# Residual columns summed by TensorE behind a normed result, the residual's update as two scalings and two adds on GpSimd

## What is computed

```python
for l in range(DEPTH):                                   # DEPTH = 2
    h = swiglu(rms_norm_2(x, ng[0]), ffn_w_gate[l, 0], ffn_w_up[l, 0], ffn_w_down[l, 0])
    x = x + 0.5 * rms_norm_2(h, ng[1])
    h = rms_norm_2(x, ng[2])
    ...
    x = x + rms_norm_2(h, ng[3])
    h = memory_xattn(rms_norm_2(x, ng[4]), mem_n, xa_wq[l], xa_wk[l], xa_wv[l], xa_wo[l])
    x = x + rms_norm_2(h, ng[5])
    h = swiglu(rms_norm_2(x, ng[6]), ffn_w_gate[l, 1], ffn_w_up[l, 1], ffn_w_down[l, 1])
    x = x + 0.5 * rms_norm_2(h, ng[7])
```

## Time and profile before

| | |
|---|---|
| median of 3 runs | 3472.39 us (3471.25 to 3475.31) |
| the profiled execution | 3471.19 us |
| its span | 3469.4 us |
| mean granted clock of TensorE | 0.918 of full speed |
| busy | PE 83%, PEld 65%, DVE 71%, ACT 22%, POOL 18% |
| HBM | 247 GB/s over the span |

### The profile page before, as it was taken

One profiled execution on the slowest core, in us unless ns is written; L12 is line 12 of the kernel. 1 busy time (PEld: TensorE's weight loads), 2 busy tenths in 40 slices (PEclk: granted clock), 3 DMA queues, 4 the chain that ended last, 5 costly groups with the idle time before them and its releaser, 6 DMA issues. The chain is left out here.

```text
span 3469.4 us, 44826 instructions
## 1 busy us (share of the span) xinstructions
PE 2896.9 (83%) x17440; PEld 2263.6 (65%) x17440; DVE 2457.6 (71%) x4625; ACT 774.4 (22%) x1982; POOL 626.5 (18%) x520
## 2 busy tenths in 40 slices
PE   8789977777777889677777779997887999998898
PEld 8678963333333689333333329987777899987798
DVE  7261677777777886877777878774436877868786
ACT  4114122222222342122222221013222101023300
POOL 0000014445444100344444440000000000000000
PEclk9899988898888899898888889998989999999999
DMA  6263559999999735899999995643203565652364
GB/s 206 87 190 99 195 209 421 410 417 414 404 401 421 260 113 171 352 414 420 417 406 389 416 391 172 192 149 128 74 5 126 170 191 173 189 172 94 123 193 142
DMA packets 469124, 859.87 MB, mean 248 GB/s; under 512 B 18736, under 2 KB 398512, under 8 KB 402224
## 3 DMA queue, kind: packets, MB, share of 16 engines
q0 software_dynamic: 73728, 536.90, 37.5%
q1 hardware_dynamic: 394896, 319.85, 29.2%
q10 hardware_dynamic: 288, 0.24, 0.0%
HBM read 848.55 MB, written 8.39 MB: 247 GB/s over the span
## 5 line engine op out<-in xcount | busy, mean ns | idle before, releaser
L2435 PE MATMUL banks<-arena,arena 128*128 128x512 f32 x1744 | 922.9, 688 | 344.4 <-ACT arena L2504 344.1
L2435 PEld LDWEIGHTS banks<-arena,arena 128*128 128x128 f32 x1744 | 374.4, 222 | 874.1 <-issue 444.6
L2393 POOL DMA_INDIRECT arena<-in_peer_uv,arena x512 | 621.5, 1214 | 1375.2 <-DVE arena L2621 681.3
L2659 DVE CUSTOM_DVE_ANT_0 arena<-arena,normed 128x1024 f32<-128x1024 f32 x512 | 625.3, 1222 | 229.1 <-DMA arena<-in_peer_uv,arena 227.0
L409 DVE TENSOR_TENSOR weight_ring_part<-weight_ring,weight_high_parts 128x2048 fp32r<-128x2048 f32 (+2 forms) x244 | 539.8, 2212 | 8.3
L3213 PE MATMUL banks<-normed_columns_part,weight_high_parts 128*128 128x256 f32 x1408 | 394.8, 280 | 3.3 <-DVE weight_ring_part L409 2.8
L3214 PE MATMUL banks<-normed_part,weight_high_parts 128*128 128x256 f32 x1408 | 392.6, 279 | 0.0
L3215 PE MATMUL banks<-normed_columns_part,weight_ring_part 128*128 128x256 f32 x1408 | 392.3, 279 | 0.0
L753 PE MATMUL banks<-weight_high_parts,arena_part 128*128 128x256 f32 x1216 | 342.6, 282 | 36.6 <-PEq L349 23.8
L406 DVE CAST weight_high_parts<-weight_ring 128x2048 fp32r<-128x2048 f32 (+2 forms) x244 | 289.6, 1187 | 104.2 <-PE banks L755 83.8
L754 PE MATMUL banks<-weight_ring_part,arena_part 128*128 128x256 f32 x1216 | 340.1, 280 | 0.0
(11 more groups left out here) (569 smaller groups left out, 4283.5 us busy)
## 6 DMA issues: line engine op xcount, KB each, us to landing
weight_ring<-in_ffn_w_gate SPq DMA_DIRECT2D x88, 512.0 KB, 3.7
weight_ring<-in_ffn_w_up SPq DMA_DIRECT2D x88, 512.0 KB, 4.9
weight_ring<-in_ev_w_in SPq DMA_DIRECT2D x33, 1024.0 KB, 5.4
weight_ring<-in_ffn_w_down SPq DMA_DIRECT2D x32, 1024.0 KB, 5.2
weight_ring<-in_od_w_in SPq DMA_DIRECT2D x23, 1024.0 KB, 5.3
weight_ring<-in_xa_wkv SPq DMA_DIRECT2D x16, 1024.0 KB, 5.3
weight_ring<-in_peer_wq SPq DMA_DIRECT2D x16, 1024.0 KB, 5.3
weight_ring<-in_ev_w_out SPq DMA_DIRECT2D x12, 1024.0 KB, 5.8
```

The lines of the kernel that those rows point to most:

```text
L2393: pool.indirect_dma_start(out=ring[:, slot(i, s), :], out_offset=None, in_=table, in_offset=bass.IndirectOffsetOnAxis(ap=index[:, i % 2, s ...
L2435: mm = pe.matmul(k.ps[:, 2 * b + half, :], diag[:, g % 2, s, :], v, start=n == b * PEER_TOPK, stop=n == last_mixed[b])
L2659: dve.tensor_tensor_reduce(out=ring[:, here, 0:D], in0=ring[:, here, 0:D], in1=k.xn[:, i % NB, :], scale=1.0, scalar=0.0, op0=ALU.mult, op ...
```

## The change

TensorE adds up the new columns itself: x turned by a matmul with the identity, plus the result times a diagonal matrix of its scale, in one bank (banks 2 to 5). The first three of four turns of the old x go before the wait for the scale. VectorE makes the two diagonals in place of its L845. GpSimd updates the rows of x once all turns are done: two scalings of `weighted` in place, then two adds, each over 128x1024. `weighted` moves to the arena (after `self.xn`, which now receives low parts while `weighted` is still read). In the next step's first tile, m=0 and m=1 (or both blocks of the first tile in `rows_out`) are made in turns, two chunks each as the parts come, except where `columns_out` has `follows` or `tensor_then`. The last landing keeps the update on VectorE, as two instructions of 128x1024. L827 moves ahead of the wait for the squares.

```diff
@@ land
-        weighted = self.xn[:, :, :].rearrange("p b (h d) -> p (b h) d", d=WIDTH)
+        weighted = self.take(NB * tiles, WIDTH) if post is not None else None
...
+                def turned_piece(t, i, b):
+                    return self.ps[:, TURNS + t, i * T + b * P:i * T + (b + 1) * P]
+                def turn_old(t):
+                    pe.wait_ge(self.squared.sem, self.squared.start + TURNS + t + 1)
+                    for i in range(2):
+                        for b in range(NB):
+                            c = 2 * t + i
+                            pe.matmul(turned_piece(t, i, b), self.x[:, b, c * P:(c + 1) * P], self.c("ident"),
+                                      start=i == 0 and b == 0, stop=False)
+                def turn_result(t):
+                    for i in range(2):
+                        for b in range(NB):
+                            mm = pe.matmul(turned_piece(t, i, b), weighted[:, t * NB + b, i * P:(i + 1) * P],
+                                           self.wide[:, b * P:(b + 1) * P], start=False, stop=i == 1 and b == NB - 1)
+                    mm.then_inc(self.turned.sem, 1)
...
-                    pe.wait_ge(self.landed.sem, self.landed.start + (j + 1) * NB)
-                    if post is not None:
-                        pe.wait_ge(self.squared.sem, self.squared.start + tiles * NB)
-                    self.turn(pe, j)
...
+                    for t in range(tiles - 1):
+                        turn_old(t)
+                    pe.wait_ge(self.tile_out.sem, self.tile_out.start + tiles * NB)
+                    pe.wait_ge(self.norm_diag.sem, self.norm_diag.start + NB)
+                    for t in range(tiles):
+                        if t == 2:
+                            turn_old(tiles - 1)
+                        turn_result(t)
...
+                @block.gpsimd
+                def _(pool):
...
+                    pool.wait_ge(self.turned.sem, self.turned.start + tiles)
+                    for b in range(NB):
+                        rows = weighted.rearrange("p (j b) d -> p b j d", b=NB)[:, b]
+                        pool.tensor_scalar(rows, rows, self.out_scale[:, b:b + 1], None, ALU.mult).then_inc(self.tile_out.sem, 1)
+                    for b in range(NB):
...
+                        pool.wait_ge(self.tile_out.sem, self.tile_out.start + tiles * NB + b + 1)
+                        pool.tensor_tensor(x, rows, x, ALU.add).then_inc(self.landed.sem, tiles)
...
-                for j in range(tiles):
+                if nxt is not None:
                     for b in range(NB):
-                        dve.scalar_tensor_tensor(piece(self.x, j, b), weighted[:, j * NB + b, :], self.out_scale[:, b:b + 1],
-                                                 piece(self.x, j, b), ALU.mult, ALU.add).then_inc(self.landed.sem, 1)
...
+                        dve.tensor_scalar(self.wide[:, b * P:(b + 1) * P], self.c("ident"), self.out_scale[:, b:b + 1], None,
+                                          ALU.mult).then_inc(self.norm_diag.sem, 1)
+                    for t in range(tiles):
+                        self.keep_low(dve, t, nxt, high_out, low_out, TURNS)
+                if nxt is None:
+                    dve.wait_ge(self.tile_out.sem, self.tile_out.start + tiles * NB)
+                    add_result(dve)
@@ columns_out (and alike in ffn, in rows_out by blocks)
+        paired = fresh and not follows and tensor_then is None
...
+                    if fresh and m == 0:
+                        for c in range(0, kc, 2):
                             self.column_ready(pe, c)
+                            for block in range(2 if paired else 1):
+                                product(block, (c, c + 1))
+                    elif not (paired and m == 1):
+                        product(m, range(kc))
                     if fresh and m == 1:
                         self.scale_tensor(pe)
```

More of the change, by code:

```diff
@@ L32 @@
 BANKS = 8
+TURNS = 2
 SIDE_BANKS = 2
@@ L757, in _ @@
                                 mm.then_inc(self.produced.sem, 1)
[L758 to L765 removed]
+                if post is None:
+                    pe.wait_ge(self.landed.sem, self.landed.start + tiles * NB)
+                    self.turn(pe, tiles - 1)
+                elif nxt is not None:
+                    self.behind(pe, self.landed)
+                    for t in range(tiles - 1):
[6 more added lines that the diff above has]
+                        turn_result(t)
@@ L822, in _ @@
                 done = self.vector_done
+                if unscaled:
+                    dve.tensor_scalar(self.out_mean, self.mean, EPS / factor ** 2, None, ALU.mult).then_inc(done.sem, 1)
+                    done.adds(1)
                 dve.wait_ge(self.squared.sem, self.squared.start + tiles * NB)
@@ L857, in land @@
             if post is not None:
-                self.tile_out.adds(NB * tiles)
+                self.tile_out.adds(NB * tiles + (NB if nxt is not None else 0))
                 self.out_ready.adds(1)
@@ L861, in land @@
                 self.out_inverted.adds(1)
+                if nxt is not None:
+                    self.norm_diag.adds(NB)
             if nxt is not None:
@@ L907, in _, with product @@
             def _(pe):
-                for m, (i, j) in enumerate(parts):
+                def product(m, chunks):
+                    i, j = parts[m]
+                    w_high, w_low = self.weights(pe, first + i)
+                    bank, w = self.ps[:, m % banks, 0:T], slice(j * P, (j + 1) * P)
+                    for c in chunks:
+                        pe.matmul(bank, w_high[:, c, w], high[:, c, :], start=c == 0, stop=False)
+                        pe.matmul(bank, w_high[:, c, w], low[:, c, :], start=False, stop=False)
+                        mm = pe.matmul(bank, w_low[:, c, w], high[:, c, :], start=False, stop=c == kc - 1)
+                    if c == kc - 1:
+                        mm.then_inc(self.produced.sem, 1)
+                for m in range(len(parts)):
                     if tensor_then is not None:
@@ L3199, in _, with product @@
         def _(pe):
+            def product(m, chunks):
+                w_high, w_low = k.weights(pe, first + m // 2)
+                bank, w = k.ps[:, m % BANKS, 0:T], slice(m % 2 * P, (m % 2 + 1) * P)
+                for c in chunks:
+                    pe.matmul(bank, w_high[:, c, w], high[:, c, :], start=c == 0, stop=False)
+                    pe.matmul(bank, w_high[:, c, w], low[:, c, :], start=False, stop=False)
+                    mm = pe.matmul(bank, w_low[:, c, w], high[:, c, :], start=False, stop=c == KC - 1)
+                if c == KC - 1:
+                    mm.then_inc(k.produced.sem, 1)
             for m in range(2 * FF_CHUNKS):
```

73 lines of the change are left out of this document (35 added, 38 removed).

## The result

| | before | after |
|---|---|---|
| median, side by side | 3473.85 us (3471.25 to 3488.27, 4 runs) | 3532.46 us (3530.9 to 3543.31, 4 runs) |
| profiled execution, span | 3471.19, 3469.4 us | 3530.9, 3529.1 us |
| mean granted clock | 0.918 | 0.92 |
| POOL busy | 626.5 us | 705.0 us |

The ratio is 1.0162, 95% interval 1.0137 to 1.0187: slower, as forecast, but by 59 us where 16 were forecast, and 20 us above the range's end (3512). Lines of the kernel moved: the result's reciprocal L839 is now L894, L406 and L409 are L407 and L410, L683 is L684, L695 is L696.

A forecast was written before the change was run, and what follows sets the result against it. Bound: the chain from the result's scale (L839) to the next norm's diagonals (L683), ended by VectorE's split. Seven landings at 0.8, plus 11.0 clock, minus 1.2, gave +15.4 to +16: 3488 us; range 3459 to 3512.

The forecast's parts named there:

- Turns: TensorE's 20 matmuls behind the diagonals, 0.12 us each at full clock, ending 3.3 us after the reciprocal; 5.2 at half clock.
- Column parts: ScalarE's and VectorE's parts of the new columns: last `keep_low` at 5.7 us, 2.6 us won against 8.4.
- Scalings: GpSimd's two scalings of the result rows, 128x1024 each: 1.1 us apiece, from 3.35 to 5.55 us.
- upper case: GpSimd passes at their upper bounds, 2.1 us a scaling and 3.2 an add: diagonals at 18.3 us, +45, 3517 us.
- Adds: GpSimd's two adds into the rows of x: 2.1 us each, the second ending at 11.1 us.
- Split meets it: VectorE's weight cast takes turns with GpSimd's adds: cast 7.75 to 8.95 us, second add 9.0 to 11.1, L409 beside it.
- split first: Rival: L409 runs ahead of GpSimd's second add, diagonals 3.1 us later than now, 3504 us; chance 0.18 together with slow passes.
- Clock: TensorE idles 5.7 us ahead of L695, then runs 4.2 us at half clock: 11.0 us over seven landings.
- Last landing: Landing without successor: VectorE's eight L845, 3.26 us, become two of 1.2 us each: -0.9 us.
- Pairs: Paired order of m=0 and m=1 in TensorE's next step frees nothing by itself: 0 us.
- Faster: Rival: quick GpSimd passes and the clock stays up: 3463 us, or 3455 if the cast isn't held up; chance 0.20.
- no change: Rival: GpSimd passes of 1.07 and 1.15 us, the gain eaten by the clock: +1.8, 3474 us; chance 0.20.

The follow-up runs named there:

- e4: Changed kernel with VectorE's split of the weight tile held back until GpSimd has landed the residual; 3527.27 us, ratio 1.0157.
- e14: As e4, with each GpSimd scaling of 1024 elements a row made as two of 512; 3524.86 us, one run.
- e2: Changed kernel without the two GpSimd scalings, so the unscaled result is added to x; 3479.18 us, one run.
- e5: Changed kernel with the update on VectorE in its idle time: tiles 0 to 2 before the first `keep_low`, tile 3 before the third; 3458.58 us, ratio 0.9939.
- e1: Changed kernel with the update back on VectorE, two passes of 128x1024 behind the last `keep_low`; 3478.93 us, ratio 1.0009.
- e6: Kernel before the change with only the paired order of m=0 and m=1 added; 3482.27 us, ratio 1.0008.
- e9: As e5, without the paired order of m=0 and m=1; 3458.35 us, ratio 0.9958.
- e7: Changed kernel with each GpSimd scaling as a two-tensor product, the factor repeated along the row; 3519.32 us, one run.
- e10: Changed kernel with GpSimd's scalings written to other tiles, starting with the scale instead of behind all turns; 3496.93 us, ratio 1.0066.
- e13: Changed kernel with 22 unused matmuls on TensorE before the spread in three gated layers behind a changed landing; 3536.76 us, one run.

## Why the prediction was right or wrong

The direction was right, and so was the mechanism in the main: TensorE's columns come sooner, the squares wait for GpSimd's adds, and L684 ends the chain. The size was off: 7.0 us a landing later than forecast (20.99 against 14.0). Part of the direction was luck: the 0.8 us by which the landing was to be longer hung on 1.25 us of waiting for the cast, which didn't happen; it is longer by reason of the scalings and the turns.

- **Diagonals and old turns.** 0.48 us for the two diagonals, and the twelve turns of old x behind the products cost nothing: they were over as the reciprocal began. Forecast, and so.
- **Turns.** Forecast to end at 3.3, measured 5.53 at a clock of 1.0: GpSimd starts 2.4 later. The clock was taken rightly, the count wrongly. The 0.12 came from "eight matmuls" in 1.13 us, but a row counts records, and such a float32 matmul leaves two: L754 has 224 records at 7 landings of 16 matmuls, while a transpose (L618) leaves one. The earlier trace rows is one head of the attention, for which the code issues four matmuls. The 20 behind the diagonals took 4.70 us (2711.18 to 2715.88), 0.235 each.
- **Column parts.** The last `keep_low` at 7.32 against 5.7, 1.6 later for the same reason; still ahead of the old 9.0 to 9.5. The prediction's "against 8.4" is where the last two of the old ones start; they end at 9.24.
- **Scalings. This is the step that failed:** "I take 1.1 for a scaling (reading beside writing, nearest the memset)". It is 2.85 alone (e4), 3.60 and 4.16 beside the split: 7.75 for two instead of 2.2, +5.55. Even the upper bound, 2.1, was under it: it assumed that GpSimd moves each stream at the rate of its memset, but no arithmetic of GpSimd stood in the trace, and a store of a constant bounds no arithmetic. The range fell with it: 2.85 in place of 2.1 puts its upper case 7 x 1.5 higher, at 3527, and turns until 5.53 another 7 x 2.2, at 3543.
- **Adds.** 2.1 taken, 2.33 measured (+0.4 for two). The Trainium skill, GPSIMD Engine Reference, section 3.1, was nearer: half of its 4497 ns for 2048 elements is 2.25, an estimate. Section 4.1 of the same page of the Trainium skill says of elementwise work on GpSimd that two inputs make it about twice as slow as on VectorE and that one input is roughly line-rate; e4 and e14 show otherwise, 2.85 for the scaling against 2.33 for the add.
- **Split meets it.** The cast was to be held up to over 2 us. It wasn't (1.22), nor was the subtraction: both ran beside scalings, which gave way to them and grew by 2.05. The adds, which would have excluded them (e2), came after VectorE was done. So the forecast's 1.25 us of waiting for the cast (7.75 to 9.0) was not there, the meeting cost 2.05 in another place, and "split first" is not what happened: it needed L409 ahead of the second add, at which VectorE had been idle for 5 us.
- **Clock.** Forecast 11.0, measured 13.5. The idle stretch was 10.5 us and not 5.7, and the half-clock stretch behind the spread 3.9 to 6.2 us and not 4.2; its price per microsecond, and that the slack of the third tile absorbs part, held. That the clock stays up during the turns held too. Taken in the same way, 0.9 us idle ahead of the spread cost 0.2 over the seven landings (e5), 3.3 us cost 5.3 (e1, where the clock fell at three of them), 3.9 us cost 10.1 (e2), each from one profile: so the prediction's "idle stretches of 2.8 us have always brought the clock down" did not carry over, and by these most of the 13.5 would have been there with the forecast's 5.7 too.
- **Last landing.** -0.7 for -0.9. **Pairs:** 0 for 0 (e6, e9).

Per landing: 0.8 forecast, +2.4 turns, +5.55 scalings, +0.4 adds, -1.25 for the wait for the cast makes 7.9, against 7.7 measured. Over seven landings with the clock that is 67; the 7 us that the span doesn't show lie mostly in the recurrent stage. Its shorter time is seen in a higher clock there; why the clock was higher stays open. It goes with the new landing and not with GpSimd's update or the pairs: in the 14 profiles that have TensorE's columns the same stage took 227.0 to 232.2 us, in the two that don't (the kernel before and e6) 235.5 and 235.4. The prediction had no term for it.

"Faster" and "no change" both needed GpSimd to add in 1.15 us; it takes twice that (2.33).

## What to carry to other kernels

Work moved to an idle engine is only free if that engine's duration for this very operation fits the gap: where the trace has none, a memset is no bound, and a small run of that one instruction is worth more than any estimate. Before moving work off a busy engine, look at its timeline for idle stretches inside the chain: here VectorE had 2 us waiting for the turned columns, and the same update put there (e5) made the change 0.6% faster than before instead of 1.6% slower. Count instructions by the code, not by the records of a row.

## What the runs showed of the hardware that was not expected

- On GpSimd a float32 scaling by one factor for each row (2.85 us for 1024 elements a partition, 2.5 ns each) is slower than an add of two tensors (2.33) and than the same scaling written as a product of two tensors (1.89). Factor constant or from SBUF, in place or not, one run or pieces: no difference.
- GpSimd's adds and VectorE's cast and two-input subtraction exclude each other for whole instructions, and VectorE waits as often as GpSimd (e2, e7, e10). GpSimd's scaling doesn't hold these two up; it is lengthened itself, by 2.05 us for 3.5 us of them, and by 0.70 less where the split is 0.70 shorter (fifth landing). It did lengthen VectorE's small diagonals, 0.48 to 1.34 (e10). What makes the two kinds differ was not found.
- Four float32 matmuls of 128 columns by the identity took 1.06 us at full clock (L748, eight records), four transposes of the same shape by the same matrix 0.60 (L619, four records, kernel after at 383.81); a filler of 256 columns took 0.44 (22 in 9.66 us, e13).
- Behind a landing the granted clock fell the oftener the longer TensorE had been idle, but not by that alone: behind 3.9 us or more at all seven (e2, the kernel after), behind 3.3 us of idleness or less it fell at three of seven landings (e1), behind 0.7 us or less at one of seven (e9).
